# Neighbourhood attention with seven half-size products a pair, sums of weights on GpSimd, and the context's products one place later

## The reference

```python
s     = einsum(q, k_band) * scale + bias      # band: 8 rows x 32 columns, outside the window -inf
s_ctx = einsum(q, k_c) * scale
p     = softmax(concatenate([s, s_ctx]))
o     = einsum(p_band, v_band) + einsum(p_ctx, v_c)
out   = (o * silu(z)) @ w_out                 # silu(z) = z / (1 + exp(-z))
```

## Time and profile before

| what | value |
|---|---|
| median of 3 runs | 3947.86 us (3943.45 to 6026.5) |
| the profiled execution | 3948.83 us, of which span 3947.2 us |
| PE (TensorE) busy | 3701.5 us, 94% |
| DVE (VectorE) busy | 1839.8 us, 47% |
| ACT (ScalarE) busy | 1184.8 us, 30% |
| POOL (GpSimd) busy | 142.6 us, 4% |
| mean granted clock of TensorE | 0.973 of full speed |

### The profile page before, as it was taken

One profiled execution on the slowest core, in us unless ns is written; L12 is line 12 of the kernel. 1 busy time (PEld: TensorE's weight loads), 2 busy tenths in 40 slices (PEclk: granted clock), 3 DMA queues, 4 the chain that ended last, 5 costly groups with the idle time before them and its releaser, 6 DMA issues.

```text
span 3947.2 us, 45687 instructions
## 1 busy us (share of the span) xinstructions
PE 3701.5 (94%) x16746; PEld 2363.9 (60%) x16746; DVE 1839.8 (47%) x3679; ACT 1184.8 (30%) x2200; POOL 142.6 (4%) x227
## 2 busy tenths in 40 slices
PE   5999899998889999989999999998898999999989
PEld 2445488883445888756666666665554555555544
DVE  3744363644554636434545454544115555555541
ACT  1213210102342101124444444444003444445430
POOL 6600000000000000000000000000000000000000
PEclk8998999999999999999999999998899999999999
DMA  7531333431013333411010101110111122122111
GB/s 150 143 80 49 86 107 86 107 95 47 18 48 96 96 99 94 124 38 38 27 37 27 37 29 35 32 32 22 32 53 54 54 58 58 53 58 58 53 32 53
DMA packets 456578, 246.42 MB, mean 62 GB/s; under 512 B 44272, under 2 KB 448496, under 8 KB 456464
## 3 DMA queue, kind: packets, MB, share of 16 engines
q1 hardware_dynamic: 420528, 216.28, 20.0%
q0 software_dynamic: 14144, 28.36, 2.6%
q10 hardware_dynamic: 21792, 0.22, 0.5%
HBM read 229.96 MB, written 14.80 MB: 62 GB/s over the span
## 4 chain that ended last, share of the span: by engine, by line
PE 87%; DVE 5%; ACT 4%; issue 2%; ACTq 1%; DMA 0%; DVEq 0%; SPq 0%
PE bank L471 19%; PE bank L1193 15%; PE bank L1736 13%; PE bank L333 10%; PE bank L1722 4%; PE bank L1041 3%; PE bank L1105 3%; PE bank L1758 2%; PE bank L868 2%; PE bank L1086 2%; PE bank L1704 2%; PE bank L851 1%; PE bank L1746 1%; PE bank L1350 1%; DVE rs L290 1%
## 5 line engine op out<-in xcount | busy, mean ns | idle before, releaser
L1193 PE MATMUL bank<-hT,ring 128*128 128x512 f32 (+1 forms) x1664 | 632.7, 530 | 12.8 <-ACT hT L1610 6.0
L1736 PE MATMUL bank<-hT,ring 128*128 128x512 f32 x1504 | 510.1, 491 | 1.0 <-ACT arena L1926 1.0
L1193 PEld LDWEIGHTS bank<-hT,ring 128*128 128x128 f32 x1664 | 310.5, 191 | 289.6 <-issue 277.4
L1736 PEld LDWEIGHTS bank<-hT,ring 128*128 128x128 f32 x1504 | 278.4, 190 | 218.6 <-issue 204.7
L333 PE MATMUL bank<-big,ring 128*128 128x512 f32 (+1 forms) x1024 | 391.1, 545 | 5.3 <-ACTq L354 2.2
L333 PEld LDWEIGHTS bank<-big,ring 128*128 128x128 f32 x1024 | 196.4, 192 | 198.5 <-issue 185.1
L1093 ACT ACTIVATE arena<-bank 128x512 f32<-128x512 f32 (+2 forms) x224 | 118.4, 528 | 462.0 <-PE bank L1086 461.8
L471 PE MATMUL bank<-big,arena 128*128 128x256 f32 x1024 | 228.8, 379 | 0.0
L471 PEld LDWEIGHTS bank<-big,arena 128*128 128x128 f32 x1024 | 194.6, 190 | 26.5
L1061 DVE CUSTOM_DVE_ANT_0 arena<-bank,big 128x512 f32<-128x512 f32 (+2 forms) x152 | 101.3, 666 | 202.1 <-PE bank L1041 202.1
L1953 DVE TENSOR_REDUCE cols<-bank 128x1 f32<-128x768 f32 x128 | 116.5, 952 | 152.4 <-PE bank L1704 152.3
(11 more groups left out here) (309 smaller groups left out, 5114.2 us busy)
## 6 DMA issues: line engine op xcount, KB each, us to landing
ring<-in_mlp_w SPq DMA_DIRECT2D x128, 512.0 KB, 5.6
ring<-in_a_w_in SPq DMA_DIRECT2D x64, 512.0 KB, 4.0
ring<-in_b_w_in SPq DMA_DIRECT2D x64, 512.0 KB, 4.1
ring<-in_mod_w SPq DMA_DIRECT2D x48, 512.0 KB, 4.2
ring<-in_even_w_in SPq DMA_DIRECT2D x32, 512.0 KB, 4.0
bias_d<-tb POOLq DMA_DIRECT2D x96, 128.0 KB, 3.5
big<-bias_d POOLq DMA_DIRECT2D x16, 768.0 KB, 5.4
ring<-in_a_w_out SPq DMA_DIRECT2D x16, 512.0 KB, 4.0
```

The lines of the kernel that those rows point to most:

```text
L1193: mm = pe.matmul(bk(b + n)[0:m, 0:z - a], ring[s][:, k, 0:m], (rhs or hcol)(k, a, z), start=k == 0, stop=k == kt - 1)
L1736: mm = pe.matmul(flatb[2][:, a:z], ring[s][:, k, :], hT[:, k, a:z], start=k == 0, stop=k == KT - 1)
```

## The change

For the latent tokens q and k together, and v and z together, are each computed as one product of 256 features by 512 tokens in **seven half-size products** (P1 to P7) of four matmuls of 128x128 by 256 columns. Round r = 0 makes q and k, round r = 1 v and z. The context's k and v remain plain products of eight matmuls of 256 columns (`n_context`), now one after the other in place 4, between the rounds. The four weight sums of a round are made by **GpSimd** (`n_weights`), round by round, with the pair's bias load between the two rounds. The sums of input blocks are made once, before the first turn, by VectorE (`dve_nat_sums`). ScalarE copies P1 and P5 out of PSUM; VectorE puts q, k, v and z together from PSUM (`n_u2`, `n_first_tile`, `n_second_tile`, `n_values`).

Other parts: v and z are ready later, so the last transposes of v (`v1`) and the gate's activation move into place 0 of the next turn (`n_open`), and pv, not qk, waits for v. The gate is Tanh(z/2) on ScalarE, and 0.5 (1 + tanh) z, in one VectorE instruction in place 4 and one factor in `outn`. The bias tiles are 256 wide, and the second half of the mask is one shared tile of zeros, read through a pattern with two pieces; the two memsets of L2326 are replaced by one of 256 columns.

Indentation is cut; `nth(name, per, g, n)` is the semaphore's count g * per + n after the two MLPs' counts.

```diff
+    def shaped(x):
+        return x if len(mask.shape) == 2 else x.rearrange("p (a n) -> p a n", a=mask.shape[1])
+    dve.tensor_tensor_reduce(shaped(sc[:, u % 2, 0:w]), shaped(bk(u % 2)[:, 0:w]), mask, 1.0, -3.0e38,
                              ALU.add, ALU.max, stat[:, 0, u:u + 1]).then_inc(p_mx, 1)
...
+        if ph.values:
+            ph.values(pe, p)
...
                 pe_qk(eng, ph, p, e, 0)
+                if ph.open:
+                    ph.open(who, eng, ph, p, e)
...
                 act_exp(eng, ph, p, e, u)
+                if u == 0 and ph.open:
+                    ph.open(who, eng, ph, p, e)
...
-            if on and u == 0 and ph.late:
+            if on and u == 4 and ph.late:
                 ph.late(eng, ph, p, e)
...
-n_v = flat[:, 11776:13056]
-bias = [flat[:, o:o + 3072].rearrange("p (v n) -> p v n", v=6) for o in (8192, 13056)]
-n_z = flat[:, 11264:11776]
+n_z = flat[:, 11520:12032]
+n_vc = flat[:, 15360:15616]
+n_rq = flat[:, 15616:16128]
+n_v = [part(8704, 2 * C), cz]
...
-        mm = dve.tensor_tensor(y[:, t], i0[:, t], z[:, t], ALU.mult)
+        mm = dve.scalar_tensor_tensor(out=y[:, t], in0=i0[:, t], scalar=0.5, in1=z[:, t],
+                                      op0=ALU.mult, op1=ALU.mult)
...
+nsum = {S1: tb[:, :, :].rearrange("p a b -> p (a b)")[:, 0:S], S2: part(6656, S)}
+nsum[S4], nsum[S3] = nsum[S1], nsum[S2]
...
+class Two:
+    def __init__(self, r):
+        self.r = r
+        b = [bk(2 + r), bk(3 - r)]
+        self.C, self.X, self.Y, self.Z = b[0][:, 0:H], b[0][:, H:S], b[1][:, 0:H], b[1][:, H:S]
+two = [Two(0), Two(1)]
+NPROD = {P1: ("A11", B11, "C"), P5: (S1, T1, "Y"), P6: (S2, T2, "X"), P4: ("A22", T4, "Z"),
+         P2: ("A12", B21, "C"), P3: (S4, B22, "Y"), P7: (S3, T3, "X")}
+def n_products(r, xs):
+    w = two[r]
+    acc = {"C": w.C, "X": w.X, "Y": w.Y, "Z": w.Z}
+    def f(pe, ph, g, e, u):
+        a, b = 4 * e + 2 * r, 4 * e + 2 * r + 1
+        opening = isinstance(g, int) and g == 0 and r == 0
+        for x in xs:
+            wt, t, o = NPROD[x]
+            if x == P1:
+                arrived(pe, "nat", a, u)
+                arrived(pe, "nat", b, u)
+                pe.wait_ge(m_free, nth("free", 2, g, r))
+                if opening:
+                    pe.wait_ge(n_out, pre9.k + 4)
+            if x == P5 and r == 1:
+                pe.wait_ge(ph.gd, g * 2 + 2)
+            if opening and t in (T1, T2, T4, T3):
+                pe.wait_ge(m_t, 2 * M_TOTAL["t"] + {T3: 1, T1: 2, T2: 3, T4: 4}[t])
+            if wt in nsum:
+                pe.wait_ge(m_wsum, nth("wsum", 8, g, 4 * r + wt))
+            if x == P6:
+                pe.wait_ge(m_copied, nth("copied", 4, g, 2 * r + 1))
+            if x == P4:
+                pe.wait_ge(m_copied, nth("copied", 4, g, 2 * r + 2))
+            if x == P2:
+                pe.wait_ge(m_u2, nth("u2", 2, g, r + 1))
+            if x == P7:
+                pe.wait_ge(m_c11, nth("c11", 2, g, r + 1))
+            for k in range(4):
+                if wt in nsum:
+                    lhs = nsum[wt][:, P * k:P * k + P]
+                else:
+                    lhs = {"A11": ring[a][:, k, :], "A12": ring[a][:, 4 + k, :], "A22": ring[b][:, 4 + k, :]}[wt]
+                if t in n_t:
+                    rhs = n_t[t][:, H * k:H * k + H]
+                else:
+                    rhs = {B11: hT[:, k, 0:H], T1: hT[:, k, H:S], B21: hT[:, 4 + k, 0:H],
+                           B22: hT[:, 4 + k, H:S]}[t]
+                mm = pe.matmul(acc[o], lhs, rhs, start=x in (P1, P5) and k == 0, stop=k == 3,
...
+                if x == P7 and k == 0:
+                    mm.then_inc(slab_done[a], 1)
+                if x == P7 and k == 1 and r == 1:
+                    mm.then_inc(slab_done[b], 1)
+            mm.then_inc(m_prod, 1)
+    return f
...
+def n_context(j):
+    def f(pe, ph, g, e, u):
+        s = 4 * e + j
+        arrived(pe, "nat", s, u)
+        if j == 1:
+            pe.wait_ge(m_u3, nth("u3", 2, g, 1))
+            if isinstance(g, int) and g == 0:
+                pe.wait_ge(u_c, 2 * KT)
+        for k in range(KT):
+            mm = pe.matmul(bk(2)[:, C * (j - 1):C * j], ring[s][:, k, :], hT[:, k, S:TT],
+                           start=j == 1 and k == 0, stop=k == KT - 1, skip_group_check=True)
+        mm.then_inc(slab_done[s] if j == 1 else nat.cv, 1)
+    return f
...
+def n_copied(r, x):
+    def f(act, ph, g, e, u):
+        act.wait_ge(m_prod, nth("prod", 14, g, 7 * r + (1 if x == P1 else 2)))
+        if x == P5:
+            act.wait_ge(m_c2, nth("c2", 2, g, r))
+        act.activation(np1 if x == P1 else np5, two[r].C if x == P1 else two[r].Y, ACT.Copy)\
+            .then_inc(m_copied, 1)
+    return f
...
+def n_weights(pool, r, g, e, u):
+    a, b = ring[4 * e + 2 * r], ring[4 * e + 2 * r + 1]
+    for x in (S1, S2, S4, S3):
+        pool.wait_ge(m_prod, nth("prod", 14, g, 7 * (r - 1) + {S1: P3, S2: P7, S4: 7 + P5, S3: 7 + P6}[x]))
+        if x == S1:
...
+        if x != S1:
+            pool.wait_ge(m_wsum, nth("wsum", 8, g, 4 * r + x - 1))
...
+        i0, i1, op = {S1: (block(b, 0), block(b, 4), ALU.add), S2: (nsum[S1], block(a, 0), ALU.subtract),
+                      S4: (block(a, 4), nsum[S2], ALU.subtract),
+                      S3: (block(a, 0), block(b, 0), ALU.subtract)}[x]
+        pool.tensor_tensor(nsum[x], i0, i1, op).then_inc(m_wsum, 1)
...
+def n_values(dve, ph, g, e, u):
+    dve.wait_ge(m_prod, nth("prod", 14, g, 7 + P2))
+    dve.wait_ge(ph.vt, g * 3)
+    for t in (0, 2):
+        m = dve.tensor_copy(bands(t, 0), two_bands(two[1].C, t))
+    m.then_inc(m_c11, 1)
...
+def n_u2(r):
     def f(dve, ph, g, e, u):
-        multiplied(dve, ph.name, 4 * e + j, u)
-        dve.wait_ge(ph.nr, g * 2)
-        if j == 0:
-            for t in range(4):
...
+def n_first_tile(r):
+    def f(dve, ph, g, e, u):
+        w = two[r]
+        if r == 0:
+            dve.wait_ge(m_prod, nth("prod", 14, g, P2))
+            dve.wait_ge(ph.nr, g * 2)
+            dve.tensor_copy(tiled(0), rows_(w.C)).then_inc(m_c11, 1)
+        dve.wait_ge(m_prod, nth("prod", 14, g, 7 * r + P3))
+        dve.wait_ge(m_u2, nth("u2", 2, g, r + 1))
+        if r == 0:
+            dve.tensor_tensor(tiled(4), rows_(nu2), rows_(w.Y), ALU.add).then_inc(m_c12, 1)
         else:
-            mm = dve.tensor_copy(n_raw[:, :], flatb[b // 2][:, 0:c])
-        mm.then_inc(ph.gd, 1)
+            for t in (0, 2):
+                m = dve.tensor_tensor(bands(t, 4), two_bands(nu2, t), two_bands(w.Y, t), ALU.add)
+            m.then_inc(m_c12, 1)
     return f
...
+def n_second_tile(r):
+    def f(dve, ph, g, e, u):
+        w = two[r]
+        dst = an(e, 2560, 512) if r else n_raw
+        dve.wait_ge(m_prod, nth("prod", 14, g, 7 * r + P7))
+        dve.tensor_tensor(nu3, np1, w.X, ALU.add).then_inc(m_u3, 1)
+        dve.wait_ge(m_u3, nth("u3", 2, g, r + 1))
+        dve.wait_ge(m_copied, nth("copied", 4, g, 2 * r + 2))
+        dve.tensor_tensor(dst[:, 0:H], nu3, w.Z, ALU.subtract).then_inc(m_free, 1)
+        dve.tensor_tensor(dst[:, H:S], nu3, np5, ALU.add).then_inc(m_c2, 1)
+    return f
+def n_ctx_k(dve, ph, g, e, u):
+    dve.wait_ge(ph.cv, g + 1)
+    dve.tensor_copy(n_raw[:, S:TT], bk(2)[:, 0:C]).then_inc(ph.gd, 1)
+def n_ctx_v(dve, ph, g, e, u):
+    dve.wait_ge(ph.cv, g + 1)
+    dve.wait_ge(ph.vt, g * 3)
+    dve.tensor_copy(n_vc, bk(2)[:, C:2 * C]).then_inc(ph.gd, 1)
...
+    a, z = SPANS[n]
     def f(act, ph, g, e, u):
         act.wait_ge(ph.st, g * 3 + (n + 1))
-        if n == 1:
-            act.wait_ge(ph.nr, g * 2 + 1)
...
     dve.scalar_tensor_tensor(out=an(e, 512, TT), in0=n_raw[:, :], scalar=cols[:, 8:9],
...
-                       grid(bk(2))[:, :, BAND0[t]:BAND0[t] + BAND], ACT.Copy)
-    act.activation(n_v[:, 4 * C:5 * C], bk(3)[:, 0:C], ACT.Copy).then_inc(ph.ga, 1)
-def z_act(act, ph, g, e, u):
-    multiplied(act, ph.name, 4 * e + 3, u)
-    act.wait_ge(ph.zf, g * 3)
-    act.activation(an(e, 2560, 512), bk(2), ACT.Copy).then_inc(ph.z, 1)
-    act.activation(n_z, bk(2), ACT.Exp, scale=-1.0).then_inc(ph.ga, 1)
 def z_dve(dve, ph, g, e):
-    dve.wait_ge(ph.ga, g * 2 + 2)
-    dve.tensor_scalar(n_z, n_z, 1.0, None, ALU.add).then_inc(ph.zf, 1)
-    dve.wait_ge(ph.zf, g * 3 + 1)
-    dve.reciprocal(n_z, n_z).then_inc(ph.zf, 1)
-    dve.wait_ge(ph.zf, g * 3 + 2)
-    dve.tensor_tensor(an(e, 2560, 512), an(e, 2560, 512), n_z, ALU.mult).then_inc(ph.zf, 1)
...
+VT = {"vc": (8, 10), "v0": (0, 4), "v1": (4, 8)}
 def vt_pe(x):
     def f(pe, ph, g, e, u):
-        pe.wait_ge(ph.ga, g * 2 + 1)
+        if x == "vc":
+            pe.wait_ge(ph.gd, g * 2 + 2)
+        else:
+            pe.wait_ge(m_c11, nth("c11", 2, g, 2))
...
-nat.pe = [job(0, 2, 0, 4, 8, gq), job(0, 2, 4, 8, 8, gq), job(1, 2, 0, 4, 8, gk, c=TT),
-          both_(st_pe("q", 0, 0, 0, S), job(1, 2, 4, 8, 8, gk, c=TT)), job(2, 2, 0, 4, 8, gv_, c=TT),
-          both_(st_pe("kl", 1, 1, 0, S), job(2, 2, 4, 8, 8, gv_, c=TT)),
```

(60 more changed lines are left out.)

102 lines of the change are left out of this document (64 added, 38 removed).

## The result

The changed kernel took 3875.53 us (median of 4 runs, 3875.03 to 3876.09), the kernel before 3948.01 us beside it (median of 4 runs, one of which took 6026.5 us): a ratio of 0.9824 [0.9812, 0.9836], that run left out (the two medians by themselves give 0.9816). The forecast was 3886, range 3867 to 3922, within 2%. So the time is in the range and the gain under 2%, as forecast; it was 72 us where 62 were forecast. The profiled execution took 3876.09 us, its span is 3874.2 us, 73.0 less than before.

The account below looks back on a forecast made before the run. TensorE was taken to bound the steady turns: 47.64 + 0.5 = 48.14 us, 3.64 less than 51.78, over 15 turns 54.6; with 5 (opening) and 2.2 (last turn) 61.8 us gained, giving 3886 us, range 3867 to 3922.

Parts of the forecast that it names:

- case A: The forecast itself: VectorE and TensorE tie at the turn's end; 3880 to 3896 us, chance 0.45.
- B: Rival: no stall at all in a turn; 3868 to 3880 us, chance 0.22.
- the old stall: TensorE's 1.06 us idle per turn, put at v's transposes waiting for the last square root's bank; claimed to go.
- The floor: TensorE's time for a steady turn if nothing waits: 50.74 less 3.10 for cheaper products, 47.64 us.
- the whole idle time: TensorE's 1.06 us idle per steady turn, all put at the last square root behind two table loads.
- windows named in advance: Signs in a steady window: TensorE busy 47.2 to 47.9 us, a turn 47.9 to 48.6 us.
- The tie at the turn's end: Before the next turn's scores, VectorE and TensorE each need 10.5 us; charged 0.5 us a turn, ends 0 and 2.5.
- rival C: Next pair's S1 and S2 on GpSimd each may hold VectorE 1.27 us at turn's end; 3906 or 3924, chance 0.27.
- exception to the order of starts: Earlier trace: a GpSimd sum started before a two-input VectorE operation, yet GpSimd took 1.85 us instead of 1.19.
- One place later: Context's k square root a whole place ahead of the transposes needing its bank; stall claimed gone, no separate price.
- The opening: Stretch up to the first score product: 5 us gained, ends 10 gained and 3 lost.
- The last turn: Gate's reciprocal leaves the chain, two ScalarE operations enter: 2.2 us gained, ends 0 and 4.

Follow-up runs that it names:

- e1: The changed kernel with one GpSimd wait added: the second sum of the next pair's round 0 starts only after VectorE's last step of the pair before; 3868.99 us.
- e3: The changed kernel with every GpSimd sum made twice into the same place; 3872.80 us.
- e5: The kernel before with Identity in place of Sqrt in the norms of q and k, so without the square root's table loads (output not the reference's); 3933.13 us.
- e4: The changed kernel with the context's two products and the sum of squares between them in place 3 instead of place 4; 3929.84 us.
- e8: The changed kernel with ScalarE's eight context shifts moved behind its first copies of P1 and P5 in the opening; 3868.45 us.
- e10: The changed kernel with the edits of e1 and e8 together; 3869.71 us.
- e2: The changed kernel with the eight weight sums of a pair made by VectorE instead of GpSimd; 3875.82 us.
- e9: The changed kernel itself, measured again for comparison on the same chip; 3876.77 us.
- e6: The changed kernel with Identity in place of Sqrt in the norms of q and k, so without those table loads (output not the reference's); 3871.72 us.

## Why the prediction was right in class and range, point by point

**The mechanism was right, that of case A.** That the time lies some 10 us under the forecast comes from the sizes of terms. B's range holds the time, but not by B's reason: the small stall is there, and the floor is lower. Turns are bound by TensorE, the products got cheaper, the old stall went, and a small wait for the scaling in `kn_dve` came. No matmul waits for GpSimd or for `n_values`, and no table load for the Tanh appears in the turns.

**The floor, 47.64, was mis-sized: it is 46.94** (e1, e3). The subtraction took 34.40 us of products for 31.30, from a busy time of 50.74. Two of its terms were off:
- The new products: 16 instructions take 3.46 us in the chain, 0.216 each and not 0.2173. 144 of them are 31.1 us: 0.2 less.
- The busy time of before was taken as work, and its pieces as even. Part of it went with the stall. In the chain of the earlier trace rows the transposes of v around the square root stand bare, 0.67 and 0.66 us for four, 1.55 for all ten, and one of the four "3.44" pieces of q and z takes 3.63. In e1's chain the ten transposes take 1.24. That is 0.31 for the transposes and 0.19 for the piece, 0.5 together.

With both, 50.74 - (34.59 - 31.13) - 0.31 = 46.97, which is the measured floor. e5 shows a part of the second term by itself: without the square root's table loads the same matmuls of before are busy for 50.49 us a turn (555.44 over eleven) instead of 50.74, and the first four transposes take 0.45 us instead of 0.67. The other four stay at 0.66, behind the wait that stays, and the piece at 3.63, so that piece has nothing to do with the stall; why it is longer is not shown. I also put the whole idle time at the square root; a quarter of it waits for the copy of transposed v (L2286), and stays in e5. The floor's error is 15 x 0.7 = 10.5 us, most of what the forecast missed by; it also put TensorE's busy time (47.02) and the turn (47.36) just under the windows named in advance, 47.2 to 47.9 and 47.9 to 48.6.

**The tie at the turn's end, charged 0.5, costs 0.42** (47.36 - 46.94), but for another reason. I made it a tie in length with 10.5 us on each side. e1 shows that VectorE alone is in time, by some 0.1 us, so the two lengths were counted well; what makes it late is S2. The 0.5 was charged for a lost tie, so that it came so near is luck. What costs is rival C's mechanism at a third of its price: not 1.27 us for S1 and S2 each, but 0.52 us longer for one scaling and nothing for S1. Two things limit it: the part that overlaps (S2 has 0.73 us to run when the scaling starts) and the shape of the VectorE instruction. Longer VectorE operations elsewhere in the turn, such as the scaling of q at 1.26 instead of 0.75 us, hold nobody up.
The Trainium skill ("SBUF — State Buffer", section "Who interferes with whom") says that a VectorE instruction with two SBUF inputs contends with a GpSimd instruction that reads, that one with at most one SBUF input does not, outside the modes in which VectorE uses two ports, and that the issue order decides who blocks. These traces agree: 1.54 against 1.02 us where S2 was first, 1.88 against 1.28 us on GpSimd where the scaling was first, and 1.75 us for the reciprocal under S1. The exception counts as well. The section names tensor_scalar among the operations that can enter those modes, and in e3 the division, one of these, takes up to 0.91 instead of 0.49 us beside a sum (here one of 1.27 us that started at 3307.04):
```profile
3307.69 0.90 DVE L1082 TENSOR_SCALAR arena<-arena,cols 128x512 f32<-128x512 f32 x1
```
The section also says that the other engine blocks fully. Measured is less: S2 had 0.73 us to run when the scaling started, and the scaling became 0.52 us longer. Nor is the earlier trace rows an exception to the order of starts, though GpSimd's sum started at 96.28 and the VectorE operation named there at 96.37. VectorE was already in another two-input operation, to 96.45:
```profile
94.11 2.34 DVE L928 SCALAR_TENSOR_TENSOR big<-arena,big 128x512 f32<-128x512 f32 x4 [0.35 <-ACT arena L884]
```

**"One place later" had no price of its own in the prediction.** The stall-free turn was assumed; e4 shows that the place makes 3.5 us of each turn against place 3 with place 4 left empty, 53 us in fifteen turns. It was right to take it as covered, but the text never named what it covers: the time from P7 through `n_second_tile` to the freed bank, and the squares of q.

**The opening: 5 was forecast, 0.5 came.** The failed step is "P5 waits for two sums of input blocks and P4 for all four, 1.22 us each, of which P1 and P6 cover half". Two things were left out: ScalarE's order, in which the context's shifts stand ahead of the copies of P1 and P5 (4.5 us, e8), and that the first input sum has two SBUF inputs just while S2 runs (0.8 us more). With the first of them mended (e8) the opening gains 4.9, near the 5, but P5's wait of 3.5 us stays, so the 5 was a guess that came near and no sum that was confirmed. The prediction listed the handovers there but followed only VectorE's and TensorE's order.

**The last turn: 2.2 forecast, 4.6 came, and the rest is the clock.** At equal clock the change is worth 2.3 there by the chain (28.4 against 26.1), as forecast. The other 2.2 are in the profiled execution's higher granted clock, 0.94 against 0.78, which nothing in the prediction foresaw; in e10, at 0.79, the same instructions took 32.38 us, more than before's 31.72. The table's 4.6 is luck of that execution.

The errors: 12.3 too little in the turns, 2.4 too little in the last turn (the clock), 4.5 too much in the opening, and 1 us outside the stage; together the 11 us between 61.8 and 73.0.

**Still open:** why the clock falls earlier in the last turn of e8 and e10 (and of e2) than in the changed kernel, e9, e1, e3, e4 and e6.

## What to carry to other kernels

Before work is subtracted from an engine's busy time, take the busy time apart piece by piece in the chain: bare instructions around a stall last longer, and that part goes with it. Where two engines share a path, ask which instruction starts first, not only how long each lasts; one added wait that nobody feels (e1) was worth 0.42 us in each of fifteen turns. And for a stretch without cover, write out the order of every engine, the one that only copies included.
